# Last combining stage: alpha times the residual and the expert pair's sum are added by TensorE in PSUM, and statistics and normalisation read them there

## The reference, cut to what matters

```python
DN_ALPHA = (2 * DEPTH) ** 0.25          # DEPTH = 2

def _layer_norm(x, g, b):
    mu = jnp.mean(xf, axis=-1, keepdims=True)
    var = jnp.mean(jnp.square(xf - mu), axis=-1, keepdims=True)
    return (xf - mu) * lax.rsqrt(var + LN_EPS) * g + b

def _post_norm(x, sub, g, b):
    return _layer_norm(DN_ALPHA * x + sub, g, b)
...
        xp = _post_norm(xp, _hier_moe(xp, *moe), ln_g[l, 1], ln_b[l, 1])
        xs = _post_norm(xs, _hier_moe(xs, *moe), ln_g[l, 1], ln_b[l, 1])
```

## Time and profile before

| | |
|---|---|
| median of 3 runs | 1342.57 us (1339.84 to 1347.92) |
| the profiled execution | 1343.1 us |
| its span in the profile | 1341.2 us |
| PE busy in the span | 1139.0 us (85%) |
| DVE busy | 488.2 us (36%) |
| ACT busy | 253.7 us (19%) |
| POOL busy | 186.0 us (14%) |
| the stage that the change touches | 1305.6 us to the end of the span |

### The profile page before, as it was taken

The page is one execution under the profiler, slowest core; times in us unless marked ns, Lnnn a source line. Parts: engine busy times, 40 slices in busy tenths (PEclk is TensorE's granted clock), DMA queues, the critical chain, the costliest instruction groups (busy, mean ns, idle before and its releaser), DMA issues. The chain is left out here.

```text
span 1341.2 us, 15442 instructions
## 1 busy us (share of the span) xinstructions
PE 1139.0 (85%) x5825; PEld 591.5 (44%) x5825; DVE 488.2 (36%) x1338; ACT 253.7 (19%) x548; POOL 186.0 (14%) x182
## 2 busy tenths in 40 slices
PE   7999999969999977884689998987999999778552
PEld 5874666635753322221334345544457433223110
DVE  2614755556631111113411324654775211111008
ACT  0311222411111111112411213241111111111011
POOL 0000000000011111102533542220000211111112
PEclk9999998989889988897789999998998999889885
DMA  7430301173369999995866998793916999999914
GB/s 266 159 107 1 130 1 63 72 286 162 155 259 413 419 421 420 420 386 199 318 205 244 396 360 323 304 342 106 420 50 228 358 418 419 421 420 421 387 66 159
DMA packets 84453, 358.90 MB, mean 268 GB/s; under 512 B 13828, under 2 KB 18053, under 8 KB 54422
## 3 DMA queue, kind: packets, MB, share of 16 engines
q1 hardware_dynamic: 62774, 279.63, 52.7%
q0 software_dynamic: 19520, 74.01, 14.4%
q10 hardware_dynamic: 2080, 4.19, 0.8%
HBM read 342.82 MB, written 31.16 MB: 279 GB/s over the span
## 5 line engine op out<-in xcount | busy, mean ns | idle before, releaser
L1850 PE MATMUL ahead_psum<-m_wg,top_xT 128*64 128x512 f32 x672 | 165.6, 641 | 44.6 <-DMA m_wg<-in_moe_w_gate_up 43.6
L1874 PE MATMUL n_psum_m<-m_wd,top_xT 128*64 128x512 f32 x528 | 123.9, 612 | 5.5 <-DMA m_wd<-in_moe_w_down 3.4
L1378 PE MATMUL ahead_psum<-top_wide,top_xT 128*128 128x512 f32 x240 | 112.4, 616 | 8.6 <-DVE top_X L1527 8.6
L1850 PEld LDWEIGHTS ahead_psum<-m_wg,top_xT 128*64 128x64 f32 x672 | 50.8, 147 | 152.7 <-issue 98.3
L1850 PE MATMUL ahead_psum<-top_wide,top_xT 128*64 128x512 f32 x320 | 80.1, 648 | 19.9 <-DMA top_wide<-in_moe_w_gate_up 19.9
L1912 DVE COPY top_xT<-n_psum_t 128x512 f32<-128x512 f32 x31 | 21.4, 692 | 188.3 <-PE n_psum_t L1835 188.3
L2251 PE MATMUL cd_psum_ab<-top_wide,top_xT 128*128 128x512 f32 x192 | 87.9, 611 | 0.1
L1279 POOL DMA_INDIRECT m_xg<-token_rows,m_tokof x31 | 31.5, 1018 | 373.8 <-PE n_psum_t L1835 198.7
L1921 DVE TENSOR_SCALAR e_Y<-n_psum_m,m_share 128x512 f32<-128x512 f32 x33 | 24.8, 751 | 129.7 <-PE n_psum_m L1874 129.7
L2095 POOL DMA_INDIRECT cd_kv<-in_cache_kT,top_kpages x64 | 60.6, 947 | 78.8 <-PE cd_psum_d L2293 51.0
L1378 PEld LDWEIGHTS ahead_psum<-top_wide,top_xT 128*128 128x128 f32 x240 | 45.3, 197 | 57.4 <-issue 57.3
(11 more groups left out here) (488 smaller groups left out, 1668.4 us busy)
## 6 DMA issues: line engine op xcount, KB each, us to landing
m_wg<-in_moe_w_gate_up SPq DMA_DIRECT2D x88, 1024.0 KB, 26.3
m_wd<-in_moe_w_down SPq DMA_DIRECT2D x64, 1024.0 KB
top_wide<-in_moe_w_gate_up SPq DMA_DIRECT2D x40, 1024.0 KB, 25.4
cd_kv<-in_cache_kT SPq DMA_DIRECT2D x64, 256.0 KB
m_wg<-expert_rows SPq DMA_DIRECT2D x16, 512.0 KB, 5.8
ab_w<-in_ab_w_in SPq DMA_DIRECT2D x2, 2048.0 KB, 11.7
top_wide<-in_ab_w_in SPq DMA_DIRECT2D x2, 2048.0 KB, 7.7
top_wide<-in_ab_w_out SPq DMA_DIRECT2D x2, 2048.0 KB, 8.6
```

Of the source, the lines that this page charges most:

```text
L1378: last = nc.tensor.matmul(pp[(2 * i + h) % 3][:P, :], mixT[:, k, tok0(t):tok0(t) + P], w[h][:, k, :], start=(k == 0), stop=(k == KD - 1))
L1850: last = nc.tensor.matmul(pg[i % 2][64 * a:64 * a + 64, :], xgT[i % 2][:, j, 64 * a:64 * a + 64], wg[2 * (i % NR) + a][:, j * 512:(j + 1) ...
L1874: last = nc.tensor.matmul(py[n2][64 * a:64 * a + 64, :], hT[:, j, 64 * a:64 * a + 64], wd[2 * (i % NR) + a][:, j * D + n2 * 512:j * D + (n ...
```

## The change

The sum that was made in X is made in PSUM. The four free banks become two buffers `sums` of two banks, used in turn.

- ScalarE first makes `ident_alpha`, alpha times the 128x128 identity, in the unused weight buffer.
- TensorE waits for it, runs six `idle_products`, and then `add_up(i)` for each tile: two products of `ident_alpha` with the two halves of X and two of the identity with the two halves of the pair's sum, accumulated in the tile's buffer. The first two need only X, the last two wait for `paired`. From tile 2 on, the first wait is for `normed`, that ScalarE has read the buffer two tiles back. The four products for gamma and beta now stand between `add_up(0)` and `add_up(1)`.
- VectorE loses the sum of each tile (L197) and waits for `summed` in its place; `bn_stats` reads PSUM. The last tile is treated as the others; `last_tile` is gone.
- ScalarE normalises out of PSUM into X, for all five tiles.
- GpSimd adds the pairs without waiting for `added`.

```diff
--- before.py
+++ after.py
@@ -304,9 +304,12 @@
         rstd, nmr = s.sb("rstd", [128, 5]), s.sb("nmr", [128, 5])
         y = combine_rows(E)
         line = E.wd[1][0:1, 0:2 * D]
+        ident_alpha = E.wd[2][:, 0:128]
         g, b = s.ps("g", 2 * 512), s.ps("b", 2 * 512)
-        (paired, line_in, gb_out, added, dv, var_in, root, mean_in, normed, final, stored) = (s.sem(x) for x in (
-            "paired", "line_in", "gb_out", "added", "dve_steps", "var_in", "root", "mean_in", "normed", "final", "stored"))
+        sums = [s.ps(f"s{i}", 2 * 512) for i in range(2)]
+        (paired, line_in, gb_out, dv, alpha_made, summed, var_in, root, mean_in, normed, final, stored) = (s.sem(x) for x in (
+            "paired", "line_in", "gb_out", "dve_steps", "alpha_made", "summed", "var_in", "root", "mean_in", "normed",
+            "final", "stored"))
         y_in = [s.sem(f"y_in{i}") for i in range(5)]
         block = s.block()
 
@@ -323,19 +326,47 @@
 
         @block.gpsimd
         def _(pool):
-            pair_rows(nc, pool, y, y_in, added, paired)
+            for i, (t, P) in enumerate(ORDER):
+                pool.wait_ge(y_in[t], 32)
+                nc.gpsimd.tensor_tensor(y[t][:P, 0, :], y[t][:P, 0, :], y[t][:P, 1, :], ALU.add).then_inc(paired, 1)
 
         @block.tensor
         def _(pe):
+            def add_up(i):
+                t, P = ORDER[i]
+                if i >= 2:
+                    pe.wait_ge(normed, i - 1)
+                for h in range(2):
+                    cols = slice(512 * h, 512 * h + 512)
+                    nc.tensor.matmul(sums[i % 2][:P, cols], ident_alpha[:P, :P], X[:P, t, cols], start=True, stop=False)
+                pe.wait_ge(paired, i + 1)
+                for h in range(2):
+                    cols = slice(512 * h, 512 * h + 512)
+                    last = nc.tensor.matmul(sums[i % 2][:P, cols], C("ident")[:P, :P], y[t][:P, 0, cols], start=False, stop=True)
+                last.then_inc(summed, 1)
+
+            pe.wait_ge(alpha_made, 1)
+            idle_products(nc, C, g, 6)
+            add_up(0)
             pe.wait_ge(line_in, 32)
             for h in range(4):
                 last = nc.tensor.matmul((g, b)[h // 2][:, 512 * (h % 2):512 * (h % 2) + 512], C("ones")[0:1, :],
                                         line[:, 512 * h:512 * h + 512], start=True, stop=True)
             last.then_inc(gb_out, 1)
+            for i in range(1, 5):
+                add_up(i)
 
         @block.vector
         def _(dve):
             c, V = Count(dve, dv), nc.vector
+
+            def statistics(i, t, P):
+                dve.wait_ge(summed, i + 1)
+                for h in range(2):
+                    c.add(V.bn_stats(st[:P, t, h, :], sums[i % 2][:P, h * 512:(h + 1) * 512]))
+                c.wait()
+                c.step(V.bn_aggr(mv[:P, t, :], st[:P, t, :, :].rearrange("p a b -> p (a b)")))
+                V.tensor_scalar(rstd[:P, t:t + 1], mv[:P, t, 1:2], LN_EPS, None, ALU.add).then_inc(var_in, 1)
 
             def scale(i, t, P):
                 dve.wait_ge(root, i + 1)
@@ -350,31 +381,21 @@
                 c.step(V.tensor_tensor(X[:P, t, :], X[:P, t, :], g[:P, :], ALU.mult))
                 V.tensor_tensor(X[:P, t, :], X[:P, t, :], b[:P, :], ALU.add).then_inc(final, 1)
 
-            def last_tile(i, t, P):
-                x = X[:P, t, :]
-                c.step(V.scalar_tensor_tensor(out=x, in0=x, scalar=mv[:P, t, 0:1], in1=g[:P, :], op0=ALU.subtract, op1=ALU.mult))
-                dve.wait_ge(root, i + 1)
-                c.step(V.reciprocal(rstd[:P, t:t + 1], rstd[:P, t:t + 1]))
-                V.scalar_tensor_tensor(out=x, in0=x, scalar=rstd[:P, t:t + 1], in1=b[:P, :], op0=ALU.mult, op1=ALU.add)\
-                 .then_inc(final, 1)
-
             for i, (t, P) in enumerate(ORDER):
-                sum_and_spread(nc, V, dve, c, X, y, i, t, P, st, mv, rstd, paired, added, var_in)
-                if i < 4:
-                    scale(i, t, P)
+                statistics(i, t, P)
+                scale(i, t, P)
                 if i >= 1:
                     affine(i - 1, *ORDER[i - 1])
-            last_tile(4, *ORDER[4])
+            affine(4, *ORDER[4])
 
         @block.scalar
         def _(act):
+            nc.scalar.activation(ident_alpha, C("ident"), ACT.Copy, scale=ALPHA).then_inc(alpha_made, 1)
             for i, (t, P) in enumerate(ORDER):
                 act.wait_ge(var_in, i + 1)
                 nc.scalar.activation(rstd[:P, t:t + 1], rstd[:P, t:t + 1], ACT.Sqrt).then_inc(root, 1)
-                if i == 4:
-                    break
                 act.wait_ge(mean_in, i + 1)
-                nc.scalar.activation(X[:P, t, :], X[:P, t, :], ACT.Identity, bias=nmr[:P, t:t + 1],
+                nc.scalar.activation(X[:P, t, :], sums[i % 2][:P, :], ACT.Identity, bias=nmr[:P, t:t + 1],
                                      scale=rstd[:P, t:t + 1]).then_inc(normed, 1)
```

## The result

The changed kernel takes 1353.64 us (median of six runs, 1350.01 to 1355.46), the kernel before in as many runs 1341.0 (1337.93 to 1347.92): 1.0085 times as long, with a 95% interval of 1.0061 to 1.0108. The profiled execution took 1355.46 us and its span is 1353.6. The forecast of 1354.8 is 1.2 us above the median.

A forecast was written before the change was run, and what follows sets the result against it. The last stage bounds: waiting for gamma and beta, then VectorE alone. Tile 1's sum at 1328.8 plus 21.6 ends VectorE at 1350.4, not 1338.2: +12.2 us on 1343.1 gives 1355.3, less 0.5 for the median, 1354.8; range 1346.5 to 1361.

The forecast's parts named there:

- (a): Start of TensorE's path: ScalarE's scaled identity takes 0.28 us, semaphore 0.05, first product at 1306.0, table load behind the copy.
- (b): Six idle products: clock rises after 4.6 us, middle of fifteen earlier rises (3.1 to 5.9 us); they end at 1310.95.
- (c): Tile 0 and gamma and beta, eight narrow products: clock falls after 2.3 us; 12.0 us, ending at 1322.95.
- (d): Tile 1's four full products: clock rises again after 4.6 us; 5.85 us, sum standing at 1328.8.
- VectorE behind it: After tile 1's sum: four statistics of 2.40, five gamma and beta steps of 2.38, 0.1 wait: 21.6 us.
- 685: Price in ns of VectorE's statistics, taken from SBUF for PSUM; the dearer alternative, 751, would add 0.5 us in all.
- Later sums: TensorE's sums after tile 1: 3.6 us a tile against VectorE's 4.78, each ending 1 to 2 us before VectorE wants it.
- Freed from `added` they run back to back: GpSimd's pair additions, 2.33 us each: tile 1's done by 1310.4, tile 4's by 1318.4 at most.
- Clock kept: Rival: clock stays up through tile 0 and the lines; tile 1's sum 1321.65, +5.1 us, 1347.7; chance 0.15.
- Late rise: Rival: idle products end before the clock rises, tile 0 and lines run cold; +15 us, 1357.5; chance 0.22.
- Never up: Rival: products with a mostly empty identity never raise the clock; +23.5 us, 1366; chance 0.06.
- Not slower: Rival: narrow products run side by side at 0.27 us each and the clock holds; time 1342.6; chance 0.04.

The follow-up runs named there:

- full_lines: Changed kernel with a 128-row stationary operand for the gamma and beta products only, tile 0 keeping 32 rows: stage 39.3 us against 44.6.
- tile1_first: Changed kernel with tile 1's products moved ahead of those for gamma and beta: stage 35.9 us, whole 1.0052 times the kernel before.
- full_rows: Changed kernel with 128-row stationary operands for tile 0 and for gamma and beta: stage 37.3 us, whole 1.005 times the kernel before.
- full_no_idle: Changed kernel with 128-row operands for tile 0, gamma and beta, and without the six idle products: stage 34.6 us, whole 1.0018 times the kernel before.
- mixed_full: Kernel before, with TensorE summing tiles 2 to 4, 128-row gamma and beta operands, GpSimd not waiting for `added`: stage 31.1 us, whole 0.9981 times.
- no_idle: Changed kernel without its six idle products: stage 41.9 us, whole 1.0105 times the kernel before.
- full_tile0: Changed kernel with 128-row operands for tile 0's four products only, gamma and beta keeping one row: stage 41.1 us.
- before_idle: Kernel before with six idle products put ahead of its gamma and beta products: stage 32.0 us against 32.6.

## Why the prediction was right

Step by step, forecast against the changed kernel's profile:

| step | forecast | measured |
|---|---|---|
| (a) first product | 1306.0 | 1306.35, copy 0.31 us, table load behind it |
| (b) idle products end | 1310.95, rise after 4.6 us | 1311.77, rise after 5.2 us |
| (c) tile 0 and lines end | 1322.95, fall after 2.3 us | 1322.64, fall after 3.3 us |
| (d) tile 1's sum | 1328.8, rise after 4.6 us | 1329.29, rise after 6.1 us |
| VectorE behind it | 21.6 us | 21.3 us (1329.31 to 1350.57) |
| VectorE ends | 1350.4 | 1350.57 |

The mechanism was the one named: up in the idle products, lost in the narrow ones, back within tile 1. The sizes came out near because errors offset each other, which is luck. The stage itself began 0.35 us later in this execution (1306.00 against 1305.65), which is no cost of the change: from there to the first product it is 0.35 us in forecast and measurement. The rise came later than the middle of the fifteen places both times, which cost 0.5 in (b) and 0.8 in (d); and the upper level lasted 3.3 us into the narrow products rather than the 2.3 read from the earlier trace rows, which gave back 1.1: together some 0.15, and with the later start the 0.5 by which tile 1's sum was later. VectorE's part then came out 0.3 shorter. The bounds for the rise, 3.1 and 5.9 us, were slightly narrow (2.9 in full_lines, 6.1 here), and the earlier trace rows show two of the fifteen places that they rest on. full_lines and tile1_first show that (c) was the least certain term: the same four products of tile 0 lost the clock in one and kept it in the other.

The evidence for (c) was also misread, and that its size came out near is luck too. The group of 8.29 us is not all of 32 rows: the timeline merges two shapes there. Taken apart, it is 4.17 us of 32-row products and then 128-row products of the same 128 columns. The second line and the last two, of the kernel before as well, show products with all 128 rows:

```profile
353.73 4.17 PE L1436 MATMUL n_psum_t<-m_xg,top_X 32*128 32x128 f32 x16
357.83 4.19 PE L1436 MATMUL n_psum_t<-m_xg,top_X 128*128 128x128 f32 x16
1023.59 7.90 PE L1436 MATMUL n_psum_t<-m_xg,top_X 128*128 128x128 f32 x32
1025.10:1028.30 3.20, 3.20 (x15) 3.20 (x14) 3.03 (x8) 0.00 (x0) 0.00 (x0) 0.50 0.96 371
```

The clock did fall 2.3 us into the 32-row products, but it stayed at 0.50 through the 128-row ones behind them (356.50 to 361.75 in the earlier trace rows), and at 1025.0 it was lost 1.4 us into a run of 128-row products (0.6 us of small 32-row ones stood ahead of them). In the second stream of the earlier trace rows the 0.52 is the clock coming back at 1018.2, during the 128-row part. So with 128 columns the clock was lost with few rows and with all of them, and these streams did not single out the rows. Of the prediction's rows only the lines of gamma and beta at 0.50 bore on products of 512 columns with few rows; what shows the cause is full_rows and full_no_idle.

- **VectorE.** Statistics read from PSUM take 1.28 to 1.30 us for two, as from SBUF, so 685 was right and 751 was not needed. ScalarE's normalisation out of PSUM takes 1.20 us against 1.24. A tile's step is 4.70 where I had 4.78; that is the 0.3 us of the table.
- **Later sums.** The timeline of the changed kernel for tiles 3 and 4 shows TensorE waiting for `normed`, and VectorE with no wait on `summed`:

```profile
1333.01 1.98 PE L341 MATMUL n_psum_s<-top_X,m_wd 128*128 128x512 f32 x4 [0.31 <-ACT top_X L398]
1337.69 1.98 PE L341 MATMUL n_psum_s<-top_X,m_wd 128*128 128x512 f32 x4 [0.98 <-ACT top_X L398]
1338.70 1.29 DVE L366 BATCH_NORM_STATS2 n_st<-n_psum_s 128x6 f32<-128x512 f32 x2
```

- **GpSimd: the step that failed.** "Freed from `added` they run back to back" was wrong in the changed kernel: its additions of tiles 1 and 2 wait 0.69 and 1.59 us for their transfers, and the last ends at 1320.43, not by 1318.4. It is wanted at 1337 and costs nothing. Worse is "its additions take 2.33 both with VectorE idle and beside it". The row shows one addition with VectorE idle; the others of that trace ran beside VectorE's statistics, never beside its sums, and took 2.34. The reading held only because `added` kept the addition and VectorE's sum apart; the wait was taken for mere ordering, and it also kept two operations off each other. In the changed kernel VectorE's sums are gone, and so nothing of it is seen: each addition takes 2.33 or 2.34. In mixed_full it cost 2.1 us. The prediction's time does not rest on this term, so its sum is untouched.

The timeline of GpSimd in the changed kernel, tiles 1 and 2:

```profile
1309.03 2.34 POOL L331 TENSOR_TENSOR m_wg<-m_wg 128x1024 f32<-128x1024 f32 x1 [0.69 <-DMA m_wg<-expert_rows]
1312.96 2.34 POOL L331 TENSOR_TENSOR m_wg<-m_wg 128x1024 f32<-128x1024 f32 x1 [1.59 <-DMA m_wg<-expert_rows]
```

**The rivals.** "Clock kept", +5.1, is refuted as a forecast for this kernel but describes full_rows: 37.3 - 32.6 = +4.7. The Trainium skill's account of the clock as a matter of how busy TensorE is ("TensorE: Matmul & The Clock Gate", Part 1) would have given that. The traces disagree: TensorE was busy throughout while the clock fell or stayed down (changed kernel from 1315.25, no_idle from 1304.75). "Late rise" did not occur, yet the rise at 5.2 us of 5.4 was close to it; it is what no_idle shows in tile 0 and the lines. "Never up" is out. "Not slower" needed narrow products under 0.3 us; they were 1.8 at the lower level and 0.9 at the upper, as full ones are.

## What to carry to other kernels

Work moved to an idle TensorE is priced at the clock that it will find there: look at PEclk where the work will stand, and at the rows of its stationary operands, not only at whether the engine is busy. For the products of 512 columns here, a stationary operand padded to 128 rows cost no more per product than one of one row or 32, and kept the clock; for products of 128 columns the trace shows no such thing. An order that lets useful full products raise it is worth more than idle ones ahead. When an edit makes a wait between VectorE and GpSimd unnecessary, ask first whether the wait also kept apart a VectorE operation on two SBUF operands and a GpSimd operation, and move only as many items to the new engine as it can deliver in time (here tiles 2 to 4 of 5: 28.6 us in place of 44.6).

## What the runs showed of the hardware beyond that

- TensorE busy all the time is no assurance of the upper clock: 13.75 us of products with operands of 32 rows and one row were at 0.50 throughout (no_idle), while ten us of products of the same length with 128 rows were at 1.00 (full_rows). Full rows are no assurance either: with 128 columns, 3.2 us of dense 128-row products were at 0.50 (kernel before, 1025.10).
- A clock at the upper level was lost 3.2 to 3.3 us into narrow products in the changed kernel, full_tile0 and full_lines, 3.8 us in before_idle, and not within 3.6 us in tile1_first, twice.
- The rise came 2.9 to 6.1 us after the start of full products in these runs: 2.9 in full_lines, 3.3 in tile1_first, 5.1 in full_rows, 5.2 and 6.1 in the changed kernel.
- VectorE's SCALAR_TENSOR_TENSOR on two SBUF operands and GpSimd's TENSOR_TENSOR do not run side by side: in eight overlaps one of the two was stretched each time, in seven the later one, by roughly what was left of the other. VectorE's statistics out of PSUM in the changed kernel ran beside a GpSimd addition with both at their usual length (1.28 and 2.34 us).
- The start of this stage differs by up to 15 us between executions of kernels that are the same up to it. None of the runs settles why.
